# Down-bias products moved from the last experts' scatters to a place behind expert 1, in a mixer and 32-expert MoE kernel

## What is computed

```
logits = xt @ w_router + b_router           # 32 experts
top_val, top_idx = lax.top_k(logits, 4)
gates = softmax(top_val)
...
hgu = xblk @ w_gu[e] + b_gu[e]              # 1024 -> 2048
gate = minimum(hgu[:, :D_FF], 7)
up = clip(hgu[:, D_FF:], -7, 7)
act = gate * sigmoid(1.702 * gate) * (up + 1)
return act @ w_down[e] + b_down[e]          # 1024 -> 1024
...
y = segment_sum(yb * row_gate, row_tok)     # sum over a token's 4 experts
x = x + y
```

## Time and profile before

| | |
|---|---|
| median of 3 runs | 1094.67 us |
| lowest, highest | 1093.05, 1094.97 us |
| the profiled execution | 1093.51 us |
| its span | 1091.8 us |
| PE, VectorE, ScalarE busy | 1052.6, 459.0, 173.2 us |
| read from HBM | 431.10 MB |

### The profile page before, as it was taken

One profiled execution on the slowest core, in us unless ns is written; L12 is line 12 of the kernel. 1 busy time (PEld: TensorE's weight loads), 2 busy tenths in 40 slices (PEclk: granted clock), 3 DMA queues, 4 the chain that ended last, 5 costly groups with the idle time before them and its releaser, 6 DMA issues.

```text
span 1091.8 us, 17310 instructions
## 1 busy us (share of the span) xinstructions
PE 1052.6 (96%) x7085; PEld 512.4 (47%) x7085; DVE 459.0 (42%) x778; ACT 173.2 (16%) x293; POOL 8.9 (1%) x21
## 2 busy tenths in 40 slices
PE   8999999999999999999999999999999999999995
PEld 7999975433333343344333333333443433343332
DVE  5567665233333333333333333333333333332354
ACT  5445533100000000000000000000000000000012
POOL 1000100000000000000000000000000000000000
PEclk9999999999999999999999999999999999999999
DMA  9873899999999999999999999999999999999993
GB/s 303 272 223 114 312 403 383 429 427 427 428 427 431 427 429 429 426 432 426 429 429 426 432 426 429 429 427 431 427 428 430 426 431 429 427 430 425 427 424 143
DMA packets 52480, 432.68 MB, mean 396 GB/s; under 512 B 4629, under 2 KB 21545, under 8 KB 26203
## 3 DMA queue, kind: packets, MB, share of 16 engines
q1 hardware_dynamic: 50817, 430.52, 95.0%
q10 hardware_dynamic: 1634, 1.74, 0.6%
HBM read 431.10 MB, written 1.39 MB: 396 GB/s over the span
## 4 chain that ended last, share of the span: by engine, by line
PE 64%; DMA 27%; DVE 4%; issue 4%; ACT 1%; SPq 1%; DVEq 0%; ACTq 0%
PE PS L1144 23%; PE PS L1173 17%; DMA down_ring<-in_w_down_dram 16%; DMA gu_ring<-in_w_gu_dram 11%; PE PS L912 9%; PE PS L1076 3%; PE PS L1120 2%; PE PS L943 2%; PE PS L1122 1%; PE PS L1187 1%; PE PS L1157 1%; PE PS L1155 1%; DVE pick_twice L1585 1%; PE PS L1191 1%; PE PS L863 0%
## 5 line engine op out<-in xcount | busy, mean ns | idle before, releaser
L1144 PE MATMUL PS<-gu_ring,XgT 128*64 128x512 f32 x2048 | 469.3, 599 | 3.8 <-DMA gu_ring<-in_w_gu_dram 3.6
L1144 PEld LDWEIGHTS PS<-gu_ring,XgT 128*64 128x64 f32 x2048 | 135.1, 136 | 267.1 <-issue 246.3
L1173 PE MATMUL PS<-down_ring,actT 128*64 128x512 f32 x984 | 219.5, 596 | 8.8 <-DMA down_ring<-in_w_down_dram 8.8
L1616 DVE TENSOR_TENSOR Y<-PS,Y 128x1024 f32<-128x1024 f32 (+1 forms) x96 | 117.0, 1220 | 255.2 <-PE PS L1122 255.2
L1173 PEld LDWEIGHTS PS<-down_ring,actT 128*64 128x64 f32 x984 | 67.4, 137 | 136.2 <-issue 119.0
L1647 DVE SCALAR_TENSOR_TENSOR y_low<-PS,slot_gate,y_high 128x512 fp32r<-128x512 f32 x31 | 23.3, 751 | 230.4 <-ACT y_high L799 230.4
L811 ACT ACTIVATE work<-PS 128x512 f32<-128x512 f32 x32 | 19.1, 597 | 456.3 <-PE PS L1144 456.3
L912 PE MATMUL PS<-h_high,win_high 128*128 128x264 f32 (+2 forms) x256 | 71.3, 287 | 0.0
L912 PE MATMUL PS<-h_high,win_low 128*128 128x264 f32 (+2 forms) x256 | 71.0, 286 | 0.0
L912 PE MATMUL PS<-h_low,win_high 128*128 128x264 f32 (+2 forms) x256 | 70.9, 286 | 0.0
L799 ACT ACTIVATE y_high<-PS,slot_gate 128x512 fp32r<-128x512 f32 x31 | 21.3, 687 | 257.1 <-PE PS L1173 257.1
(11 more groups left out here) (236 smaller groups left out, 780.4 us busy)
## 6 DMA issues: line engine op xcount, KB each, us to landing
gu_ring<-in_w_gu_dram SPq DMA_DIRECT2D x119, 2048.0 KB, 28.5
down_ring<-in_w_down_dram SPq DMA_DIRECT2D x60, 2048.0 KB, 21.4
gu_ring<-in_w_gu_dram SPq DMA_DIRECT2D x18, 1024.0 KB, 9.9
gu_ring<-in_w_in_dram SPq DMA_DIRECT2D x16, 1024.0 KB, 8.7
gu_ring<-in_w_down_dram SPq DMA_DIRECT2D x4, 1024.0 KB, 27.6
down_ring<-in_w_down_dram SPq DMA_DIRECT2D x3, 1024.0 KB, 9.4
down_ring<-in_w_pool_up_dram SPq DMA_DIRECT2D x1, 2048.0 KB, 11.8
gu_ring<-in_w_conv_out_dram SPq DMA_DIRECT2D x2, 1024.0 KB, 6.2
```

Of the source, the lines that this page charges most:

```text
L1144: last = mm(PS[SLOTS * h:SLOTS * h + SLOTS, b, :], XgT[:, k, :], w[:, D * b + HALF * h:D * b + HALF * h + HALF], start=(k == 0), stop=(k = ...
L1173: last = mm(PS[SLOTS * h:SLOTS * h + SLOTS, bank, :], acts[:, f % 4, f // 4, :], rows[:, f, HALF * h:HALF * h + HALF], start=(f == 0), sto ...
L1616: tt(Y[rows, t, :].rearrange("p (h n) -> p h n", h=2), PS[rows, bank:bank + 2, :], Y[rows, t, :].rearrange("p (h n) -> p h n", h=2), ALU.a ...
```

## The change

The bias pair is taken out of `scatter`. A new function, `scatter_bias(t)`, makes the same two matmuls into banks of its own list, `BIAS_BANKS` (6 and 7, 0 and 1, 6 and 7), as a finished product, and raises `bd_done`. It is called three times around the end of expert 1's item: for t = 0 behind `down(0)` and ahead of `turn(1)`, and for t = 1 and 2 behind `turn(1)`. The one for t = 2 waits for the addition of t = 0, which used the same banks; TensorE enters the loop only when the addition of t = 1 is made (`added` 3), since gate/up writes banks 0 and 1. On VectorE a new function, `add_bias(t)`, adds each product to Y, behind expert 1's item and ahead of the loop. All later waits on `added` count 3 more. As no scatter differs from the others any more, experts 28 and 29 run in TensorE's loop, and 30 and 31 stay written out.

```diff
--- before.py
+++ after.py
@@ -40,6 +40,7 @@
 FILL = (2, 3)
 TAILS = PBUF + CBUF + 2 * SAMPLE
 NEAR = META - CBUF
+BIAS_BANKS = (6, 0, 6)
 MARK = -1e38
 GONE = -3e38
 LOGIT_BANKS = (1, 2, 4)
@@ -846,7 +847,7 @@
             act.wait_ge(scattered, more * (3 * E) + 3 * (E - 1))
             high(last, slot_gate_last, 5)
             for t in range(NT):
-                act.wait_ge(added, more * (3 * E) + (3 * (E - 1) + t + 2))
+                act.wait_ge(added, more * (3 * E) + (3 * (E - 1) + t + 5))
                 root(4 + t, t, gu_ring[0:P if t < 2 else SAMPLE, 5 + t, 0:D])
 
         @block.tensor
@@ -1110,25 +1111,28 @@
                     last = gather_parts(k, ((0, 0), (2, 0), (4, 0), (1, 1), (3, 1), (5, 1), (6, 2)), True, True)
                 last.then_inc(gathered, 1)
 
-            def scatter(t, way=spread, bank=6, bias=False):
+            def scatter(t, way=spread, bank=6):
                 halves = [(h, slice(SLOTS * h, SLOTS * h + SLOTS)) for h in range(2)]
-                if bias:
-                    for h, _ in halves:
-                        mm(PS[:, bank + h, :], GT[t], bdown_rows[t][:, HALF * h:HALF * h + HALF],
-                           start=True, stop=False)
                 for h, rows in halves:
-                    mm(PS[:, bank + h, :], way[rows, t, :], y_high[rows, :], start=not bias, stop=False)
+                    mm(PS[:, bank + h, :], way[rows, t, :], y_high[rows, :], start=True, stop=False)
                 for h, rows in halves:
                     last = mm(PS[:, bank + h, :], way[rows, t, :], y_low[rows, :], start=False, stop=True)
                 last.then_inc(scattered, 1)
 
-            def scatter_item(i, t, bias=False):
+            def scatter_item(i, t):
                 if t == 0:
                     pe.wait_ge(low_ready, i + 1)
-                pe.wait_ge(added, 3 * i + (t + 1))
-                scatter(t, bias=bias)
-
-            def gate_up(i, u, landed, two_before, bias=None):
+                pe.wait_ge(added, 3 * i + (t + 4))
+                scatter(t)
+
+            def scatter_bias(t):
+                if t == 2:
+                    pe.wait_ge(added, 2)
+                for h in range(2):
+                    last = mm(PS[:, BIAS_BANKS[t] + h, :], GT[t], bdown_rows[t][:, HALF * h:HALF * h + HALF], start=True, stop=True)
+                last.then_inc(bd_done, 1)
+
+            def gate_up(i, u, landed, two_before):
 
                 by_halves = type(i) is int and i == 0
                 pe.wait_ge(*((first_half_ready, 1) if by_halves else (xg_ready, i + 1)))
@@ -1146,7 +1150,7 @@
                                       start=(k == 0), stop=(k == KT - 1))
                     last.then_inc(gu_used, 1)
                     if two_before is not None and k in (2, 4, 6):
-                        scatter_item(two_before, k // 2 - 1, bias == k // 2 - 1)
+                        scatter_item(two_before, k // 2 - 1)
 
             def way_back(i, bank=4):
 
@@ -1191,14 +1195,18 @@
                     last = nc.tensor.transpose(PS[:, 3, P * j:P * j + P], by_j[:, 1, j, :], ident[:])
                 last.then_inc(up_turned, 1)
 
-            def item(i, u, landed, before=None, two_before=None, bias=None):
-                gate_up(i, u, landed, two_before, bias)
+            def item(i, u, landed, before=None, two_before=None):
+                gate_up(i, u, landed, two_before)
                 if before is not None:
                     way_back(before)
                 pe.wait_ge(pick_ready, i + 2)
                 gather()
                 if before is not None:
                     down(before, beside=(type(before) is int and before == 0))
+                if type(before) is int and before == 0:
+                    pe.wait_ge(gt_kept, NT + 1)
+                    pe.wait_ge(late_landed, 80)
+                    scatter_bias(0)
                 turn(i)
 
             gate_up(0, 0, 32, None)
@@ -1208,10 +1216,13 @@
             gather()
             turn(0)
             item(1, 1, 32, 0)
+            scatter_bias(1)
+            scatter_bias(2)
+            pe.wait_ge(added, 3)
             pe.wait_ge(next_landed, 16)
             pe.wait_ge(more_ready, 1)
             more = pe.value_load(more_sb[0:1, 0:1], min_val=0, max_val=ROUNDS - 1)
-            with pe.Fori(0, more * (E // 2) + (E // 2 - 3)) as pair:
+            with pe.Fori(0, more * (E // 2) + (E // 2 - 2)) as pair:
                 item(2 * pair + 2, 0, 16 * pair + 48, 2 * pair + 1, 2 * pair)
                 item(2 * pair + 3, 1, 16 * pair + 48, 2 * pair + 2, 2 * pair + 1)
 
@@ -1220,22 +1231,18 @@
 
             last, before, two_before = from_end(1), from_end(2), from_end(3)
             landed = more * (8 * E) + (8 * E + 16)
-            pe.wait_ge(gt_kept, NT + 1)
-            pe.wait_ge(late_landed, 80)
-            item(from_end(4), 0, more * (8 * E) + 8 * E, from_end(5), from_end(6), bias=0)
-            item(two_before, 1, more * (8 * E) + 8 * E, from_end(4), from_end(5), bias=1)
-            item(before, 0, landed, two_before, from_end(4), bias=2)
+            item(before, 0, landed, two_before, from_end(4))
 
             gate_up(last, 1, landed, two_before)
             way_back(before)
             turn(last)
             down(before)
             way_back(last, 5)
-            pe.wait_ge(added, more * (3 * E) + (3 * (E - 3) + 4))
+            pe.wait_ge(added, more * (3 * E) + (3 * (E - 3) + 7))
             down(last, down_last, last_landed, 5, before, act_last)
             pe.wait_ge(low_ready, last + 1)
             for t in range(NT):
-                pe.wait_ge(added, more * (3 * E) + (3 * (E - 2) + t + 2))
+                pe.wait_ge(added, more * (3 * E) + (3 * (E - 2) + t + 5))
                 scatter(t, spread_last, LAST_BANKS[t])
 
         @block.vector
@@ -1670,8 +1677,16 @@
                 if after is not None and before is not None:
                     low_part(before)
 
+            def add_bias(t):
+                rows = slice(0, P if t < 2 else SAMPLE)
+                v.wait_ge(bd_done, t + 1)
+                tt(Y[rows, t, :].rearrange("p (h n) -> p h n", h=2), PS[rows, BIAS_BANKS[t]:BIAS_BANKS[t] + 2, :],
+                   Y[rows, t, :].rearrange("p (h n) -> p h n", h=2), ALU.add).then_inc(added, 1)
+
             item(0, 1)
             item(1, 2, 0)
+            for t in range(NT):
+                add_bias(t)
             with v.Fori(0, more * E + (E - 3)) as m:
                 item(m + 2, m + 3, m + 1, (m + 1) % E, m)
             last, before, two_before = more * E + (E - 1), more * E + (E - 2), more * E + (E - 3)
```

## The result

| | before | changed |
|---|---|---|
| median of 8 runs each | 1093.22 us | 1096.81 us |
| lowest, highest | 1091.64, 1094.97 us | 1094.96, 1098.29 us |
| ratio, 95% interval | | 1.0029 [1.0020, 1.0037] |
| profiled execution, its span | 1093.51, 1091.8 us | 1098.29, 1096.6 us |

The change makes the kernel slower by 0.29%, about 3.2 us. That is inside the range but not where most of the chance lay: a loss of over 2.2 us had 0.22. The profiled execution of the changed kernel is its highest; it stands 4.8 us over that of before.

The account below looks back on a forecast made before the run. The prediction took the stream of weights as the bound: 0 for removed pairs, 0 for PE's delay and 0.6 us for the stream gave +0.6 us, so 1095.3 us on a median of 1094.67, range 1093.3 to 1098.0.

Parts of the forecast that it names:

- The stream is the bound: Whole kernel: weight loads need 29.4 us per expert, PE 27.6; removing 5.7 us of pairs before 1052.98 gains nothing.
- PE is 6.2 us late: Start of expert 2's gate/up: about 223.7 instead of 217.56, from added pairs, an addition and the register load.
- The upper bound of 8 us: Upper bound on PE's delay at expert 2, if each of two new waits adds some 0.9 us more.
- PE's own delay costs nothing: PE after expert 2 starts: its 6.2 us delay is taken up by 8.8 us of down-load waits before 748 us.
- the 5.6 us forecast: PE's waits for down loads: a sign that they would shrink by about 5.6 us in total.
- a cushion of about 1.2 + 1.0 = 2.2 us: DMA queue: lead over the previous landing that an issue needs; at 1.75 us some 0.5 us is lost.
- predicted (1.75): Issue of expert 4's first load at 227.45: 1.75 us ahead of the previous landing at 229.2, 8.0 before.
- the dip at 177.67: Load issued at 177.67 with a 1.2 us cushion: DMA share fell, 1.0 us lost, taken as the model.
- the 9.5 us: Shortest issue-to-landing of a 2048 KB gate/up load; with it expert 4's first load would lose 2.9 us.
- the sum: Whole kernel: 0 for removed pairs, 0 for PE's delay, 0.6 us for the stream, giving +0.6 us.
- the stream starves for longer: Rival at expert 4's first load: too short a queue delays the stream by 2.9 us, 1097.6 us; chance 0.22.
- "wrong" case: Profile sign: DMA share clearly under 1.0 over more than 1 us behind 228, last landing later by as much.

Follow-up runs that it names:

- e3: Changed kernel without any bias pair or addition, leaving out the product with b_down: 1092.42 us over 1093.11 of the kernel before, ratio 0.9991.
- e2: Changed kernel with the bias pair for t = 1 in banks 4 and 5, no wait for its addition before the loop: 1093.18 over 1093.11 us, ratio 1.0002.
- e10: Kernel before with nineteen useless matmuls (4.1 us) between experts 1 and 2: 1094.09 us over 1093.97, ratio 1.0006.
- e1: Changed kernel with ten useless matmuls filling TensorE's 2.24 us idle stretch: 1095.14 us over 1093.11 of the kernel before, ratio 1.0021.
- e4: Kernel before with thirty useless matmuls (6.4 us) between experts 1 and 2: 1095.14 us over 1093.11, ratio 1.0021.
- e5: Changed kernel measured once more, nothing altered: 1096.53 us over 1093.01 of the kernel before, ratio 1.0029.
- e9: Changed kernel with bias pairs replaced by 9, 9 and 1 matmuls of 128 rows: 1095.45 us over 1093.97 of the kernel before, ratio 1.0014.
- e6: Changed kernel with TensorE's round-count load moved ahead of the pairs for t = 1 and 2: 1095.43 us over 1093.01 of the kernel before, ratio 1.0023.
- e8: Changed kernel with bias pairs replaced by 9, 5 and 5 matmuls of 128 rows: 1094.63 us over 1093.01 of the kernel before, ratio 1.0013.

## Why the prediction was right and wrong

- **The stream is the bound, and what PE saves ahead of 1052.98 is paid out as waiting: right.** e3 gives 0.7 us of 5.7.
- **"PE is 6.2 us late": 6.35 measured, but by two errors that cancel.** The pairs of t = 1 and 2 took 2.2 us together, not 3.8: cheaper by 1.6. For the same reason pair 2 no longer covered the addition of t = 1, and PE idled 2.24 us where 0.4 were reckoned (223.7 less 223.29). The register load behind the addition, 1.1 us, was right. The upper bound of 8 us took 0.9 us more for each new wait; no run shows that term, gate/up started 0.1 us behind the loop's registers.
- **PE's own delay costs nothing: right** as far as runs show it: 4 us of it cost nothing (e2, e10). Its waits for down loads shrank by less than the 5.6 us forecast, from 8.8 to 7.5 us, since the stream was late as well.
- **"So the engines want a cushion of about 1.2 + 1.0 = 2.2 us": this step failed.** It is 3.5 us or more. In e1 and e4 the cushion was 1.6 and 1.5 us, as predicted (1.75), and 2.0 us were lost, not 0.5; by their own landings it was 2.5 and 1.8, in e1 above the 2.2 that should have been enough. The 2.2 came from the dip at 177.67, read as a share over 1.5 us. The same dip of the kernel before over 6 us:

```profile
176.00:182.00 6.00, 6.00 (x30) 2.01 (x28) 4.86 (x22) 1.95 (x3) 0.00 (x0) 1.00 0.82 276
```

By the share 1.1 us are missing, by the bytes (276 GB/s of 428) 2.1 us. The time lost lies between the two where it was measured (e1 over 217 to 240: 1.6 by the share, 2.9 by the bytes, 2.0 us of time). So this dip asks for a cushion of anything from 2.3 to 3.3 us, and the prediction took the lowest reading for the answer. I also took landings as the time at which the engines run dry. They run dry earlier: in the changed kernel the share falls at 226, while the last load landed at 228.8, and after the issue at 229.68 no data come until past 230. The estimate in the prediction from the Trainium skill, "DMA: Bandwidth & Descriptors", section "Anatomy of one DMA — SWDGE (gpsimd) path", was 6.8 us to landing and 0.2 us of loss. The loads issued 2.5 us or less ahead of the landing before them took 7.5 to 7.8 us (e4: 8.9), and e1, with 7.6, lost 2.0. So neither that estimate nor the 9.5 us was the time on a drained queue. With 3.5 us the sum would have been 1.75 us of loss before any word on the clock, at the very edge of "the same".
- **Missing from the sum: the clock.** I priced the idle stretch at its own length. With it PE's clock was halved for 3.4 and 6.8 us in the two profiled executions; that moved the issue by 1.4 to 2.7 us (from gate/up to issue 5.09 us in e5 and 6.41 in the changed kernel, 3.69 in e1), and cost some 1.5 us of the median (1096.5 to 1096.8 against e1's 1095.1). The prediction says that nothing covers the pairs on PE, and never asks at what speed PE goes on behind a wait.
- **The rival "the stream starves for longer" is what happened.** Its mechanism was right. That its price (2.9 us) came close is luck: by delay alone it was 2.0 us, the clock made up the rest, and the 9.5 us are not what a load takes on a drained queue. It was given 0.22 because the dip at 177.67 "was 1.0 us only", that is, on one row read too narrowly. The range holds the result only because this rival set its upper end.
- **The forecast time hides half of the miss.** 1095.3 stands 1.5 us from 1096.81, but a change of +0.6 us was forecast and +3.6 came. The median of three runs that it was put on, 1094.67, was 1.45 us above that of eight, 1093.22. That is luck, too.
- **2.0 us of starving and about 1.5 us of clock** are the measured 3.2 (ratio) to 3.6 us (medians). The 2.0 were measured apart (e1, e4); the 1.5 are the difference.
- Of the signs: last load and last chunk came late as the "wrong" case said (share under 1.0 for more than 1 us, the last landing later by as much); the tail of 38.8 us and the missing bias matmuls at 955 to 1026 were as said.

## What to carry to other kernels

When a stream of loads is the bound, a delay of the consuming engine is free only until the issue that it holds back comes too late: measure by how much the loads' queue is ahead at that issue, and test it with filler of known length (here nothing lost at 4 us, 2.0 us at 6, 4.4 us at 9). Work placed on TensorE's path can cost less than the wait that comes with it: here a pair of banks that nothing waits for took away the wait, the halved clock and the whole loss (e2). And when a wait on TensorE is added, price what follows it too.

## What the runs showed of the hardware

- The granted clock of TensorE fell from 1.00 to 0.50 around an idle stretch of 2.24 us in the middle of a program that had run at 1.00 throughout, and came back after 3.4 us (e5) or 6.8 us (changed kernel), in two executions of the same code, and after 3.4 us in e9. With idle stretches of 1.37 us (e6), 1.39 us (e8) and 1.73 us (the kernel before, ahead of 1079.89, clock 1.00 from 1075 to 1085) the profiled executions show no fall. Nor does the kernel before at its very start, where TensorE waits 3.35 us for a load and the clock stands at 1.00 over the first 5 us; so an idle stretch is not followed by the fall every time.
- Two bias pairs behind one another ran in 2.20 us where one pair takes 1.91 us. Their operands lie in different groups of 32 rows, and their weight loads stand packed in one row of 1.37 us; between the loads of a single pair there are gaps. The Trainium skill, "TensorE: Matmul & The Clock Gate", section "Part 3: Packing small matmuls — row/col tiling", says that small products in different groups of rows run side by side; this trace agrees, with 2.20 us for two against 1.91 for one, and the prediction had passed it over. What makes them overlap was not tried apart.
- In the changed kernel the share falls to 0.35 behind 226, in windows of a quarter microsecond it is zero for good from 227.75, and the load lands at 228.8: its last data come 1.0 us ahead of the landing, most of them over 2 us ahead. After the issue at 229.68 the first data stand past 230.5, some 0.8 us later. What is lost while the queue runs out (1.3 us from 226 to 227.75), the 1.0 and the 0.8 together are an estimated 3.1 us, most of what the stream wants.
- A 2048 KB load of this stream took 7.5 to 7.8 us to landing on a drained or nearly drained queue (e1, e5 to e9 and the changed kernel; 8.9 in e4), against 12.8 us for the same load in the kernel before.
